# A two-layer decoder trunk on one core: a split weight block written in halves, row-scale transposes moved by one tile, the last FFN chunk of layer 1 computed channel-major, and a re-cut final normalisation

## What is computed

```python
for layer in range(2):
    xn = rms_norm(h, norm_mix_g[layer])
    ...                       # layer 0: causal pooling + differential attention; layer 1: conv module + block attention
    h = h + mix
    hn = rms_norm(h, norm_ffn_g[layer])
    h = h + (silu(hn @ w_gate[layer]) * (hn @ w_up[layer])) @ w_down[layer]    # d_ff = 2816
return rms_norm(h, norm_final_g)
```

## Time and profile before

| | |
|---|---|
| Median of 3 runs | 579.51 us (579.14 to 580.39) |
| Profiled execution, its own time | 579.54 us |
| Span in its profile | 577.3 us |
| TensorE busy | 568.4 us (98%) |
| VectorE busy | 408.5 us (71%) |
| ScalarE busy | 278.6 us (48%) |
| Mean granted TensorE clock | 0.998 |

### The profile page before, as it was taken

One profiled execution on the slowest core, in us unless ns is written; L12 is line 12 of the kernel. 1 busy time (PEld: TensorE's weight loads), 2 busy tenths in 40 slices (PEclk: granted clock), 3 DMA queues, 4 the chain that ended last, 5 costly groups with the idle time before them and its releaser, 6 DMA issues.

```text
span 577.3 us, 8426 instructions
## 1 busy us (share of the span) xinstructions
PE 568.4 (98%) x3159; PEld 491.1 (85%) x3159; DVE 408.5 (71%) x546; ACT 278.6 (48%) x395; POOL 15.5 (3%) x55
## 2 busy tenths in 40 slices
PE   8999999999999999999999999999999999999995
PEld 7899988788888888888889999888888888888884
DVE  6579995775666777667777999767476666677753
ACT  6688665544343443444456345544444444344322
POOL 1200001000000000000000000000000000000000
PEclk9999999999999999999999999999999999999999
DMA  8986444463566645448468541623745446665401
GB/s 307 329 304 197 161 145 146 146 225 112 178 215 218 218 165 181 173 160 303 146 207 297 188 147 55 207 104 125 239 154 171 173 168 207 218 217 179 149 0 73
DMA packets 30408, 105.50 MB, mean 183 GB/s; under 512 B 3376, under 2 KB 4144, under 8 KB 30384
## 3 DMA queue, kind: packets, MB, share of 16 engines
q1 hardware_dynamic: 30096, 104.91, 53.2%
q10 hardware_dynamic: 288, 0.27, 0.2%
HBM read 104.11 MB, written 1.05 MB: 182 GB/s over the span
## 4 chain that ended last, share of the span: by engine, by line
PE 86%; DVE 4%; DMA 3%; issue 3%; SPq 2%; ACT 1%; POOL 0%; POOLq 0%; DVEq 0%; ACTq 0%
PE bank L1647 20%; PE bank L1251 17%; PE bank L1253 17%; PE bank L1252 17%; PE bank L1650 11%; DMA raw<-in_slabs 3%; DVE w_lo L776 2%; PE bank L1320 1%; PE bank L1419 1%; PE bank L1616 0%; SPq L331 0%; PE bank L1445 0%; PE bank L1406 0%; DVE h L824 0%; SPq L335 0%
## 5 line engine op out<-in xcount | busy, mean ns | idle before, releaser
L776 DVE TENSOR_TENSOR w_lo<-raw,w_hi 128x2048 fp32r<-128x2048 f32 (+2 forms) x95 | 211.4, 2227 | 20.8 <-ACT w_hi L444 20.8
L444 ACT ACTIVATE w_hi<-raw 128x2048 fp32r<-128x2048 f32 x91 | 173.2, 1910 | 11.4 <-DMA raw<-in_slabs 6.5
L1647 PE MATMUL bank<-xT,w_hi 128*128 128x512 f32 x512 | 128.0, 392 | 0.0
L1647 PEld LDWEIGHTS bank<-xT,w_hi 128*128 128x128 f32 x512 | 92.9, 189 | 17.2
L1251 PE MATMUL bank<-w_lo,yT_hi 128*128 128x512 f32 x240 | 95.5, 398 | 0.0
L1253 PE MATMUL bank<-w_hi,yT_lo 128*128 128x512 f32 x240 | 93.6, 390 | 0.0
L1252 PE MATMUL bank<-w_hi,yT_hi 128*128 128x512 f32 x240 | 93.6, 390 | 0.0
L1171 DVE TENSOR_REDUCE work<-bank 128x512 f32<-128x1024 f32 x32 | 39.0, 1220 | 77.0 <-PE bank L1650 77.0
L1650 PEld LDWEIGHTS bank<-xT,w_lo 128*128 128x128 f32 x512 | 69.8, 190 | 5.0
L1650 PE MATMUL bank<-xT,w_lo 128*128 128x256 f32 x512 | 71.4, 282 | 0.0
L689 ACT ACTIVATE work<-work 128x256 f32<-128x256 f32 x32 | 13.4, 419 | 97.2 <-DVE work L1171 97.2
(11 more groups left out here) (177 smaller groups left out, 595.0 us busy)
## 6 DMA issues: line engine op xcount, KB each, us to landing
raw<-in_slabs SPq DMA_DIRECT2D x186, 512.0 KB, 4.6
raw<-in_slabs SPq DMA_DIRECT2D x6, 256.0 KB, 5.6
h<-in_x SPq DMA_DIRECT2D x2, 512.0 KB, 8.0
gain<-in_norm_ffn_g SPq DMA_DIRECT2D x2, 512.0 KB, 7.2
out<-h SPq DMA_DIRECT2D x4, 256.0 KB, 2.0
raw<-in_slabs SPq DMA_DIRECT2D x4, 128.0 KB, 5.3
h<-in_x_cols SPq DMA_DIRECT2D x1, 512.0 KB, 5.6
gain<-in_norm_mix_g SPq DMA_DIRECT2D x1, 512.0 KB, 6.0
```

Source lines behind the costliest of these rows:

```text
L444: A(w_hi[:, t % SLOTS, :], raw[:, t % RAW_SLOTS, :], ACT.Copy).then_inc(hi_ready, 1)
L776: V.tensor_tensor(w_lo[:, t % SLOTS, c], raw[:, t % RAW_SLOTS, c], w_hi[:, t % SLOTS, c].bitcast(F32), ALU.subtract).then_inc(lo_ready, 1)
L1647: T.matmul(bank[:, b + m, :], hi, xT[:, k, :, :, :], start=k == 0, stop=False)
```

## The change

Six edits. (1) At the FFN entry of layer 0 the low part of slab f+2 is written by two instructions of half the width, each ahead of one block of `norm_lo`. (2) `rstd_rows` is moved behind the next tile of 24 products. (3) The last chunk of layer 1's FFN is channel-major, and its two slabs are laid out so on the host; the last slab's products are ordered anew: half 0 by channel block, half 1's columns 0 to 511 before its columns 512 to 1023, and of these the last slab's part in two pieces of 256 columns, the last one into bank 4. (4) The columns 0 to 511 of half 1 are added while half 0 waits for its power; ScalarE squares columns 0 to 767 of half 1 in two instructions, VectorE adds, squares and sums the last 256. (5) ScalarE scales columns 0 to 511 of half 1 from `gained`, VectorE the other 512 in two pieces by the row scale and the gain at once. (6) The last two stores are 128 x 256 and 128 x 768. Layer 0 keeps its last chunk as it was (those lines, only indented, are left out).

```diff
-  for half in range(HALVES):
-      for b in range(2):
-          c = slice(b * HALFD, (b + 1) * HALFD)
-          sp.wait_ge((normed, last_scaled)[b], (norm_no(4) + 1 + half, 1 + half)[b])
-          sp.dma_start(out[half * P:(half + 1) * P, c], h[:, half, c]).then_inc(out_stored, 16)
+  for b in range(2):
+      c = slice(b * HALFD, (b + 1) * HALFD)
+      sp.wait_ge((normed, last_scaled)[b], (norm_no(4) + 1, 1)[b])
+      sp.dma_start(out[0:P, c], h[:, 0, c]).then_inc(out_stored, 16)
+  sp.wait_ge(normed, norm_no(4) + 2)
+  sp.dma_start(out[P:2 * P, 3 * D // 4:], h[:, 1, 3 * D // 4:]).then_inc(out_stored, 16)
+  sp.wait_ge(normed, norm_no(4) + 3)
+  sp.wait_ge(last_scaled, 2)
+  sp.dma_start(out[P:2 * P, 0:3 * D // 4], h[:, 1, 0:3 * D // 4]).then_inc(out_stored, 16)
...
+  def last_squares():
+      for n, c in enumerate((slice(0, HALFD), slice(HALFD, HALFD + 256))):
+          act.wait_ge(h_added, 15 + n)
+          act.wait_ge(squared, 18 + n)
+          A(xn[:, c], h[:, 1, c], ACT.Square, scale=float(D) ** -0.5, accum_out=sumsq[:, 2 + n:3 + n])\
+              .then_inc(squared, 1)
-      act.wait_ge(gain_used, 2 * half + 2)
-      A(h[:, half, HALFD:], gained[:, 1, :], ACT.Copy, scale=rstd[:, half:half + 1])\
-          .then_inc(last_scaled, 1)
+      act.wait_ge(gain_used, 2 + half)
+      c = slice(0, HALFD) if half else slice(HALFD, 2 * HALFD)
+      A(h[:, half, c], gained[:, 1 - half, :], ACT.Copy, scale=rstd[:, half:half + 1]).then_inc(last_scaled, 1)
...
+      else:
+          split_his(nxt - 1)
+          gate_tanh(2 * last, 0)
+          act_hi(2 * last, 0, last % 2)
+          gate_tanh(2 * last + 1, 1)
+          act_hi(2 * last + 1, 1, last % 2)
+          norm_squares(st, 0)
           last_scale(0)
-      norm_squares(st, 1)
-      if l == 1:
+          last_squares()
           last_scale(1)
...
+  def split_lo_half(s, n):
+      dve.wait_ge(hi_ready, s + 1)
+      c = slice(n * SLAB // 2, (n + 1) * SLAB // 2)
+      part = V.tensor_tensor(w_lo[:, s % SLOTS, c], raw[:, s % RAW_SLOTS, c],
+                             w_hi[:, s % SLOTS, c].bitcast(F32), ALU.subtract)
+      if n:
+          part.then_inc(lo_ready, 1)
...
-              if half:
-                  dve.wait_ge((normed, last_scaled)[b], (norm_no(4) + 1, 1)[b])
...
+      if meanwhile:
+          meanwhile()
...
+  def first_columns():
+      dve.wait_ge(acc_done, 12)
+      V.tensor_tensor(h[:, 1, 0:HALFD], bank[:, 2, :], h[:, 1, 0:HALFD], ALU.add).then_inc(h_added, 1)
+  def last_columns():
+      edge = slice(HALFD + 256, 2 * HALFD)
+      dve.wait_ge(h_added, 15)
+      dve.wait_ge(normed, norm_no(4) + 1)
+      V.tensor_tensor(gained[:, 0, :], h[:, 1, 0:HALFD], gain[:, 0:HALFD], ALU.mult).then_inc(gain_used, 1)
+      dve.wait_ge(squared, 19)
+      V.tensor_scalar(meansq[:, 1:2], sumsq[:, 2:3], EPS, None, ALU.add).then_inc(dve_chain, 1)
+      chain[0] += 1
+      dve.wait_ge(edge_done, 1)
+      V.tensor_tensor(h[:, 1, HALFD:], bank[:, 3, :], h[:, 1, HALFD:], ALU.add).then_inc(h_added, 1)
+      dve.wait_ge(slab_used, SLABS)
+      dve.wait_ge(h_added, 16)
+      V.tensor_tensor(h[:, 1, edge], bank[:, 4, 0:256], h[:, 1, edge], ALU.add).then_inc(h_added, 1)
+      dve.wait_ge(h_added, 17)
+      link(V.scalar_tensor_tensor(xn[:, edge], h[:, 1, edge], 1.0 / D, h[:, 1, edge], ALU.mult, ALU.mult,
+                                  accum_out=sumsq[:, 4:5]))
+      dve.wait_ge(squared, 20)
+      V.tensor_scalar(meansq[:, 1:2], meansq[:, 1:2], sumsq[:, 3:4], sumsq[:, 4:5], ALU.add, ALU.add)\
+          .then_inc(pow_asked, 1)
+      dve.wait_ge(pow_done, pow_no("norm", 4, 1))
+      for c in (slice(3 * D // 4, D), slice(HALFD, 3 * D // 4)):
+          V.scalar_tensor_tensor(h[:, 1, c], h[:, 1, c], rstd[:, 1:2], gain[:, c],
                                  ALU.mult, ALU.mult).then_inc(normed, 1)
       norm_scale(2 * l + 1, 0)
-      norm_lo(2 * l + 1, 0)
       if l == 0:
-          split_los(f + 2)
+          for b in range(2):
+              split_lo_half(f + 2, b)
+              norm_lo(2 * l + 1, 0, (b,))
           norm_add(2 * l + 1, 1)
           split_los(f + 3)
           norm_scale(2 * l + 1, 1)
       else:
+          norm_lo(2 * l + 1, 0)
           norm_add(2 * l + 1, 1)
           norm_scale(2 * l + 1, 1)
           split_los(f + 3)
...
+      else:
+          split_los(nxt - 1)
+          pair_sum(last, 0)
+          swiglu(2 * last, 0)
+          act_lo(2 * last, 0, last % 2)
+          pair_sum(last, 1)
+          swiglu(2 * last + 1, 1)
+          act_lo(2 * last + 1, 1, last % 2)
+          norm_add(st, 0)
+          norm_scale(st, 0, first_columns)
+          last_columns()
...
       qk_tile(0, 0, 2, kb, 0, first)
       qk_tile(0, 0, 0, q0, 0, first)
       qk_tile(0, 0, 2, kb, 0, second)
+      qk_tile(0, 0, 3, kb, 256).then_inc(k_done, 1)
       rstd_rows()
-      qk_tile(0, 0, 3, kb, 256).then_inc(k_done, 1)
       qk_tile(0, 0, 0, q0, 0, second).then_inc(q_done, 1)
       pool_transposes()
       qk_tile(0, 0, 1, q1, 0, release=True)
...
+      else:
+          pe.wait_ge(act_ready, U + 2 * e - 1)
+          pair(up_slab(l, e), up_slab(l, e), 4)
+          pe.wait_ge(at_lo, U + 2 * e)
+          pair(up_slab(l, e) + 1, up_slab(l, e) + 1, 6)
+          down(e - 1, 2 * e - 1, down_slab(l, e - 1), 0, (e - 1) % 2)
+          a_hi, a_lo = (t[:, 0, 2 * (e % 2):2 * (e % 2) + 2, :] for t in (actT_hi, actT_lo))
+          pe.wait_ge(lo_ready, SLABS)
+          for k in range(2):
+              pe.wait_ge(at_lo, U + 2 * e + 1 + k)
+              for b in range(2):
+                  hi, lo = w_part(down_slab(l, e), k * D + b * HALFD, HALFD)
+                  last = split_product(bank[:, b, :], a_hi[:, k, :], a_lo[:, k, :], hi, lo, False, k == 1)
+                  if k == 1:
+                      last.then_inc(acc_done, 1)
+          down(e - 1, 2 * e - 1, down_slab(l, e - 1), 1, (e - 1) % 2, blocks=(0,))
+          down(e, 2 * e + 1, down_slab(l, e), 1, e % 2, final=True, blocks=(0,))
+          down(e - 1, 2 * e - 1, down_slab(l, e - 1), 1, (e - 1) % 2, blocks=(1,))
+          a_hi, a_lo = (t[:, 1, 2 * (e % 2):2 * (e % 2) + 2, :] for t in (actT_hi, actT_lo))
+          for c in (0, 256):
+              for k in range(2):
+                  hi, lo = w_part(down_slab(l, e), k * D + HALFD + c, 256)
+                  o = bank[:, 4, 0:256] if c else bank[:, 3, 0:256]
+                  last = split_product(o, a_hi[:, k, :], a_lo[:, k, :], hi, lo, c > 0 and k == 0, k == 1)
+              last.then_inc(slab_used if c else edge_done, 1)
...
-  if i in (0, 1, 10):
+  if i in (0, 1) or (l, i) == (0, 10):
       slabs += [columns(k0, 4, (gate, 256 * i, 256), (up, 256 * i, 256)) for k0 in (0, 4)]
   else:
       slabs += [columns(0, 8, (gate, c, 128), (up, c, 128)) for c in (256 * i, 256 * i + 128)]
```

More of the change, by code:

```diff
@@ L719, in ffn_act @@
                 nxt, st = f + 3 * NCH, 2 * l + 2
[L720 to L725, removed]
-                if l == 0:
[L727 to L731, removed]
-                if l == 1:
+                if l == 0:
+                    split_his(nxt - 1)
+                    tanh(last, 0, 0)
+                    split_his(nxt, nxt + 1)
+                    norm_squares(st, 0)
+                    split_his(nxt + 2)
+                    tanh(last, 1, 1)
+                    if l == 0:
+                        norm_hi(st, 0, (0,))
+                    at_hi_evac(2 * last + 1, 1, last % 2, 1)
+                    if l == 0:
+                        norm_hi(st, 0, (1,))
+                    split_his(nxt + 3)
+                    norm_squares(st, 1)
+                else:
+                    split_his(nxt - 1)
+                    gate_tanh(2 * last, 0)
+                    act_hi(2 * last, 0, last % 2)
+                    gate_tanh(2 * last + 1, 1)
+                    act_hi(2 * last + 1, 1, last % 2)
+                    norm_squares(st, 0)
                     last_scale(0)
-                norm_squares(st, 1)
-                if l == 1:
+                    last_squares()
                     last_scale(1)
@@ L827, in norm_add, with norm_scale @@
                         dve.wait_ge(h_added, 4 * (st - 1) + 2 * half + b + 1)
-                        if half:
-                            dve.wait_ge((normed, last_scaled)[b], (norm_no(4) + 1, 1)[b])
                         V.tensor_tensor(gained[:, b, :], hp, gain[:, b * HALFD:(b + 1) * HALFD],
                                         ALU.mult).then_inc(gain_used, 1)
-            def norm_scale(st, half):
+            def norm_scale(st, half, meanwhile=None):
                 n = 4 * st + 2 * half
@@ L1205, in ffn_dve @@
                 nxt, st = f + 3 * NCH, 2 * l + 2
[L1206 to L1214, removed]
@@ L1618, in transposes, with down @@
                     last.then_inc(act_t, 1)
-                def down(i, n, static, half, ip, first=False, final=False, between=None):
```

(26 more changed lines are left out.)

34 lines of the change are left out of this document (23 added, 11 removed).

## The result

Six runs of each kernel on one chip: 577.82 us median (577.39 to 578.30) for the changed kernel against 580.05 us (579.14 to 580.47) for the one before, ratio 0.9961, 95% interval 0.9951 to 0.9972. The change takes 2.2 us off. The prediction was 577.5 us, within 576.7 to 578.5.

What follows compares the result with a forecast made beforehand. TensorE's program plus its pauses, and the stretch after its last product, were taken to bound the kernel. Edit 1's 0.9, edit 2's 0 and edits 3 to 6's 1.1 sum to 2.0 us off 579.54: 577.5, range 576.7 to 578.5.

Steps and rivals of the forecast that it cites:

- Edit 1: Layer 0's FFN entry: half-width low parts fill two VectorE gaps, removing TensorE's 0.90 us pause at half 1's transposes.
- Edit 2: Row scales one tile later: TensorE's 0.4 us pause goes but it waits longer for probabilities; 0, bounds -0.4 and 0.
- What I said a profile would show: For edit 2: no TensorE wait for row scales at line 813, and the wait for line 901 grown to 0.6.
- Edit 3: Layer 1's last chunk channel-major, without transposes: the last product starts at 570.27 instead of 570.77, 0.50 us earlier.
- the 0.88 us above the 95 steps: Layer 1's last chunk before the change: time beyond 95 product steps of 0.228 us, taken as two sets of transposes.
- The new wait for `act_lo`: Last slab's second channel block: activation takes 3.7 us, TensorE has 4.1 us of products meanwhile; holds by 0.4 us.
- Edits 4 to 6: Tail: second of the last stores issued at about 573.45 against 574.6, -1.15 us; edits 3 to 6 together -1.1.
- VectorE's readiness: Tail: VectorE finishes its earlier work at 569.95, about when the first 256 columns' end is signalled, 569.88.
- Half speed for the square: Rival: VectorE's square with sum in the tail runs at half speed, some 0.25 us more, 577.8; chance 0.15.
- a late `act_lo`: Rival: TensorE waits 2.3 us for `act_lo` in layer 1's last chunk, 579.8, slower than before; chance 0.04.
- The late VectorE in the tail: Rival: half 0's norm and half 1's first block queue on VectorE, 0.5 us more, 578.0; chance 0.06.
- the halves in vain: Rival: the half-width low parts don't remove the FFN-entry pause, edit 1 gives 0, 578.4; chance 0.06.

Runs made afterwards that it cites:

- the three runs on this edit: Slab f+2's low part whole behind `norm_lo` in the changed kernel, 0.9966; edit 1 alone on the kernel before, 0.9975; whole ahead in the changed kernel, 0.9979.
- the changed kernel's second profile: The changed kernel run once more, unedited: median 577.72 us, ratio 0.9959 to the kernel before.
- the cover: Removed from the changed kernel: 12 instead of 18 products run during the second group's activation, the last slab's half 0 going block by block; 578.91 us, ratio 0.9971.

## Why the prediction was right

- **What bounds it.** TensorE's program plus its pauses plus the tail: the span became 2.1 us shorter, of which the three distances give 1.10 + 0.54 + 0.57 = 2.21, less 0.11 for the later A.
- **Edit 1**, forecast 0.9 (bounds 0 to 1.0), measured 0.97 to 1.10. The mechanism was as put, and the three runs on this edit show it: gaps of 1.17 and 1.12 us filled, the add at 102.95 (forecast 102.9), no new wait for the high part of f+3. The term was a little small because 8 transposes in a row without a wait took 0.79 us, not the 0.88 read off the chain in the earlier trace rows.
- **Edit 2**, forecast 0, measured nothing that shows, with the open end told above. The reason given (ScalarE's own queue and the wait at the probabilities) held for the profile of the kernel before, and one more half tile of delay cost 0.69 us. It is not so in every run: in seven of the thirteen profiles TensorE's own path decides, where a pause would have counted in full; the two of them with the row scales early had none. What I said a profile would show was only half right: the wait at line 1492 grew from 0.6 to 0.8 in all, but in the changed kernel's second profile it is 0.5.
- **Edit 3.** The last product was forecast 0.50 us earlier within the chunk, measured 0.54. In the list of waits I had passed over the largest, 1.7 us for the identity matrix at the kernel's start, which no edit touches, and the 1.3 us at line 1616. Of the latter the last chunk's two sets of transposes held 0.9; the sum had them, inside the 0.88 us above the 95 steps. The new wait for `act_lo` held with 0.4 us, as put; taking the cover away cost 1.1.
- **Edits 4 to 6.** From the last product to the last store 3.18 us were forecast (573.45 - 570.27), and 3.22 measured. VectorE was ready at 568.75, and by the forecast's own 0.33 us behind the start of its last product (568.52) the first piece ended at 568.85: both met, as forecast. The nearness of 3.18 and 3.22 is partly luck: the last sum came 1.33 us after the last product's start instead of 1.46, the scaling then 0.93 us later instead of 0.88, and the last store 0.96 us behind that instead of 0.84. The terms given for VectorE's readiness also add up to 570.01 and not to 569.95.
- **Half speed for the square** (0.15) fell: 0.42 us with the sum, 0.418 without. The Trainium skill, "Vector Engine (DVE) Microarchitecture Reference", "Points that are easy to get wrong", has such an instruction with two non-bf16 sources at half throughput; this form, two f32 operands of 256 columns, does not bear that out. The sum costs a second instruction of 0.08 us; the Trainium skill, "VectorE: DVE Perf Modes", "Two Vector instructions with no wait between them", says that such an operation is two instructions, and the trace agrees. The term of 0.1 us for it was, if anything, too large: from the square's start to the last sum it is 0.47 us, 0.52 in the forecast.
- The rival that ended slower, a late `act_lo` with 2.3 us of wait, did not come about. Without the cover it waits 1.1 us, and that kernel is still faster than the one before (0.9971). The late VectorE in the tail and the halves in vain did not come about.

The predicted 577.5 rests on the profiled run's 579.54; over all runs the kernel before had a median of 580.05, and the difference of 2.2 us is the better comparison with the forecast 2.0. The missing 0.2 is edit 1's, as far as one pair of profiles shows. That the median lies only 0.3 us from 577.5 is partly luck: the forecast started from a profiled run 0.5 us below the median of the six, and the gain was 0.2 us larger than forecast.

## What to carry to other kernels

Look for the gaps that a helper engine has inside its own chain, measure them, and cut a long independent instruction to their size; put whole in front of the chain, the same instruction costs what it saved. A pause of the bounding engine is worth something only if the point where it next meets the others isn't set by them: compare the time of that meeting point with each path to it, in more than one run. In a tail of short steps, count hand-overs: giving a one-column root to the engine that applies it was worth 0.40 us, as much as re-cutting adds, squares and stores (0.38).

## What was not expected of the hardware

- The first transfers arrive at other times in every run, and with them the first 256-column product moves between 27.76 and 29.00 us and, with the run of the row scales moved later left out, A between 98.73 and 99.88. That is about as much as the executions of one kernel differ by (580.05 us median, 579.14 to 580.47).
- TensorE's products of 512 columns follow each other at 0.227 us and those of 256 at 0.119 to 0.120 with a new weight block each, so halving the width of the last products costs 0.17 us in twelve.
- VectorE reads its sum in 0.08 us; ScalarE takes 0.19.
- A root of one column on ScalarE takes 0.20 us, its table 1.28 us once; on GpSimd the power takes 0.55.
